# Hybrid decoder step on one Trainium2 core: dense projections as plain float32 matmuls instead of three split products

## The reference

```python
def layer(x, ...):
    h = rmsnorm(x, norm1_w)
    z = h @ w_in                     # 1024 -> 2 x 8 x 128 columns less 96: q, k, v, gates, latents, conv input
    y_ret = retention(...)           # 4 heads, chunks of 128, with a recurrent state
    y_mla = latent_attention(...)    # 8 heads; the 8 new tokens attend to 2048 cached positions in pages
    y_rg  = rg_lru(...)              # conv of width 4, gates, a scan
    x = x + concat([y_ret, y_mla, y_rg]) @ w_out          # 1024 -> 1024
    up = rmsnorm(x, norm2_w) @ w_up                       # 1024 -> 2 x 2816
    gate, val = split(up)
    x = x + (silu(causal_conv3(gate)) * val) @ w_down     # 2816 -> 1024
# after two layers: y = rmsnorm(x, final_w)
```

## Time and profile before

| | |
|---|---|
| median of 3 runs | 1723.7 us (1722.09 to 1728.46) |
| profiled execution, span | 1725.0 us |
| PE busy | 1541.2 us, 89% |
| weight loads busy | 1390.6 us, 81% |
| DVE busy | 882.3 us, 51% |
| ACT busy | 532.0 us, 31% |
| HBM read | 141.24 MB |
| mean granted TensorE clock | 0.895 |

### The profile page before, as it was taken

How to read it: one execution, slowest core, us unless ns; L and a number is a source line. 1 busy time by engine, 2 the same in 40 slices (tenths; PEclk the granted TensorE clock), 3 DMA queues, 4 the chain that set the end, 5 groups by cost and what they waited for, 6 DMA issues and landing times.

```text
span 1725.0 us, 31192 instructions
## 1 busy us (share of the span) xinstructions
PE 1541.2 (89%) x11052; PEld 1390.6 (81%) x11052; DVE 882.3 (51%) x1454; ACT 532.0 (31%) x778; POOL 24.7 (1%) x49
## 2 busy tenths in 40 slices
PE   4988797778999999999999888878899999999993
PEld 4988565446999999999998786544588999999993
DVE  4584142433476653666566812443336666356664
ACT  3340022322344422333423301222224443223341
POOL 1000000000000000000000000000000000000001
PEclk9996576889999999999999955778899999999997
DMA  7310212123222223222352012222232222232221
GB/s 274 117 56 26 82 49 79 45 68 98 89 71 86 89 85 107 85 97 71 106 185 89 21 55 65 69 59 70 72 105 73 89 87 82 95 99 87 79 92 50
DMA packets 119422, 146.72 MB, mean 85 GB/s; under 512 B 16609, under 2 KB 90626, under 8 KB 119202
## 3 DMA queue, kind: packets, MB, share of 16 engines
q1 hardware_dynamic: 116114, 133.54, 24.5%
q0 software_dynamic: 3216, 12.00, 2.0%
HBM read 141.24 MB, written 4.45 MB: 84 GB/s over the span
## 4 chain that ended last, share of the span: by engine, by line
PE 78%; DVE 8%; issue 7%; ACT 3%; SPq 2%; DMA 1%; DVEq 0%; ACTq 0%; POOL 0%; POOLq 0%
PE PS L1230 56%; PE PS L1508 4%; PE PS L1334 4%; PE PS L1459 2%; PE PS L1531 2%; PE PS L1332 1%; SPq L336 1%; SPq L341 1%; DVE STAT L1022 1%; PE PS L1245 1%; PE PS L1445 1%; PE PS L1383 1%; PE PS L1386 1%; ACT PR L643 1%; DVE R L840 1%
## 5 line engine op out<-in xcount | busy, mean ns | idle before, releaser
L1230 PE MATMUL PS<-XNH,WH 128*128 128x260 f32 x2176 | 445.7, 286 | 48.3 <-DVE WL L739 33.2
L1230 PE MATMUL PS<-XNH,WL 128*128 128x260 f32 x2176 | 442.6, 285 | 0.0
L1230 PE MATMUL PS<-XNL,WH 128*128 128x260 f32 x2176 | 442.1, 285 | 0.0
L1230 PEld LDWEIGHTS PS<-XNH,WH 128*128 128x128 f32 x2176 | 339.2, 190 | 52.4 <-issue 38.2
L452 ACT ACTIVATE WH<-RAW 128x1024 fp32r<-128x1024 f32 x200 | 211.5, 1058 | 435.7 <-PE PS L1230 360.2
L1230 PEld LDWEIGHTS PS<-XNH,WL 128*128 128x128 f32 x2176 | 338.4, 190 | 0.3
L1230 PEld LDWEIGHTS PS<-XNL,WH 128*128 128x128 f32 x2176 | 337.8, 190 | 0.4
L739 DVE TENSOR_TENSOR WL<-RAW,WH 128x1024 fp32r<-128x1024 f32 x200 | 244.5, 1222 | 168.7 <-ACT WH L452 162.3
L1230 PE MATMUL PS<-HL,WH 128*128 128x260 f32 x704 | 141.9, 283 | 0.0
L1230 PE MATMUL PS<-HH,WL 128*128 128x260 f32 x704 | 141.5, 282 | 0.0
L1230 PE MATMUL PS<-HH,WH 128*128 128x260 f32 x704 | 141.3, 282 | 0.0
(11 more groups left out here) (246 smaller groups left out, 1453.9 us busy)
## 6 DMA issues: line engine op xcount, KB each, us to landing
RAW<-in_units SPq DMA_DIRECT2D x134, 512.0 KB, 3.3
KT<-in_kat SPq DMA_DIRECT2D x256, 64.0 KB, 1.8
KT<-in_ka SPq DMA_DIRECT2D x256, 64.0 KB, 1.9
RAW<-in_units SPq DMA_DIRECT2D x32, 384.0 KB, 3.0
RAW<-in_units SPq DMA_DIRECT2D x32, 320.0 KB, 2.9
RT<-in_kar SPq DMA_DIRECT2D x256, 16.0 KB, 1.7
C<-in_const POOLq DMA_DIRECT2D x1, 2228.0 KB, 10.1
X<-in_x SPq DMA_DIRECT2D x8, 260.0 KB, 4.3
```

What stands on the lines that cost most here:

```text
L1230: last = mm(PS[i % 4][0:rows, hb, 0:HB], w, x(kk)[:, hb * HB:(hb + 1) * HB], start=(kk == 0 and s == 0), stop=(kk == total - 1 and s == 2))
```

## The change

The dense projections are done by plain float32 matmuls on the raw weights: two per weight tile and chunk instead of six. WH, WL, XNL and HL are gone, XNH becomes XN, HH becomes H, and RAW becomes W with seven slots. `hi` and `lo` and all the subtractions are removed. SP loads a unit when the product seven units back is done (UNIT_USE names the tile that uses a unit). The buffers that lay over the raw slots and the split buffers (PD, O8, SMALL, C8, QD, SS, KC) have places of their own. The first product and the first up product wait for XN chunk by chunk, the first down product of a half for each H tile. ACT alone empties the mixed outputs. The layer loops and inner loops are unrolled in Python, and CREDIT is gone.

```diff
-NRAW, NHL = 4, 2
+NW_SLOTS = 7
+UNIT_USE = [(f"in{z}", None) for z in ORDER] + [(f"wo{m}", None) for m in range(KD)]
+for _i, (_j0, _n) in enumerate(HALVES):
+    UNIT_USE += [(f"up{_i}_{j}", None) for j in range(2 * _n)]
+    for _m in range(KD):
+        UNIT_USE += [(f"dn{_i}_{_m}", KD * _i + _m + 1), (f"dn{_i}_{_m}", None)]
...
+        def wait_weights(e, l, u):
+            n = l * N_UNITS + u
+            e.wait_ge(w_full[n % NW_SLOTS], 16 * (n // NW_SLOTS + 1))
+
+        def wait_unit_used(e, l, u):
+            name, half = UNIT_USE[u]
+            if half is None:
+                wait_full(e, l, name)
+            else:
+                wait(e, "mid_used", l, half)
...
             def one(l, u, width=UW):
-                unit_wait(l, u)
-                src = units[bass.ds(l * N_UNITS + u, 1), :, 0:width].rearrange("a p n -> p (a n)")
-                sp.dma_start(RAW[:, u % NRAW, 0:width], src).then_inc(raw_full[u % NRAW], 16)
+                n = l * N_UNITS + u
+                if n >= NW_SLOTS:
+                    wait_unit_used(sp, *divmod(n - NW_SLOTS, N_UNITS))
+                sp.dma_start(W[:, n % NW_SLOTS, 0:width], units[n, :, 0:width]).then_inc(w_full[n % NW_SLOTS], 16)
...
-            with sp.Fori(0, DEPTH) as l:
-                for u in range(NRAW + 1):
+            for l in range(DEPTH):
+                for u in range(4):
                     one(l, u)
...
-                for u in range(NRAW + 1, N_IN_U + 2):
+                for u in range(4, N_IN_U):
                     one(l, u, 256 if u == U_KR else UW)
-                    g = u - (NRAW + 1)
+                    g = u - 4
                     if g < 2 * (N_PAGES // 4):
                         four_pages(l, 0, 0, g // 4, 4 * (g % 4))
-                with sp.Fori(0, NB // 2 - 1) as bp:
+                for u in range(N_IN_U, N_IN_U + NW_SLOTS):
+                    one(l, u)
+                for bp in range(NB // 2 - 1):
                     pages(l, 0, bp + 1)
-                with sp.Fori(0, NB // 2) as bp:
+                for bp in range(NB // 2):
                     pages(l, 1, bp)
-                wait_full(sp, l, "dy")
-                settle(sp)
-                for u in range(N_IN_U + 2, U_UP[0]):
+                for u in range(N_IN_U + NW_SLOTS, U_UP[0]):
                     one(l, u)
...
-            def hi(l, u, it=None, tile=None, mid=None):
...
-                act.activation(WH[:, u % NHL, :], RAW[:, u % NRAW, :], ACT.Copy).then_inc(hi_split[u % NHL], 1)
...
-            def lo(l, u, it=None, per=0):
...
-                V_.tensor_tensor(WL[:, u % NHL, :], RAW[:, u % NRAW, :], WH[:, u % NHL, :].bitcast(F32), ALU.subtract)\
-                    .then_inc(lo_split[u % NHL], 1)
...
-                remainder(l, c0, k, weight)
-
-            def remainder(l, c0, k, weight):
-                wait(dve, "xh_ready", l, c0 + k + 1)
-                V_.scalar_tensor_tensor(XNL[:, k, :], X[:, k, :], weight, XNH[:, k, :].bitcast(F32), ALU.mult, ALU.subtract)\
-                    .then_inc(S["xl_ready"][0], 1)
...
-                        act.activation(XNH[r, 2 + g // 2, 0:SEQ], ps(f"o{g}")[r, 0, :], ACT.Copy).then_inc(S["mix_hi"][0], 1)
+                        act.activation(XN[r, 2 + g // 2, 0:SEQ], ps(f"o{g}")[r, 0, :], ACT.Copy).then_inc(emptied(f"o{g}"), 1)
...
-                            V_.scalar_tensor_tensor(two(HF[:, jj, :]), two(TH[:, jj, :]), 0.5, PS[vi % 4][:, :, 0:HB],
+                            V_.scalar_tensor_tensor(two(H[:, it * 2 + jj, :]), two(TH[:, jj, :]), 0.5, PS[vi % 4][:, :, 0:HB],
                                                     ALU.mult, ALU.mult).then_inc(emptied_s[vi % 4], 1)
-                            lo(l, U_UP[hf] + 2 * jj + 3, it, 4)
-                            wait(dve, "hh_ready", l, c + 1)
-                            hsl = bass.ds(it * 2 + jj, 1)
-                            V_.tensor_tensor(HL[:, hsl, :], HF[:, jj:jj + 1, :], HH[:, hsl, :].bitcast(F32), ALU.subtract)\
-                                .then_inc(S["hl_ready"][0], 1)
...
+            def product(l, name, us, x, rows=P, ready=None):
+                wait_tile(pe, l, name)
+                total, kk = sum(n for _, n in us), 0
                 for u, n in us:
...
+                    wait_weights(pe, l, u)
+                    slot = (l * N_UNITS + u) % NW_SLOTS
                     for k in range(n):
...
-                        for s, (w, x) in enumerate(((wh, xh), (wh, xl), (wl, xh))):
-                            for hb in range(2):
-                                last = mm(PS[i % 4][0:rows, hb, 0:HB], w, x(kk)[:, hb * HB:(hb + 1) * HB],
-                                          start=(kk == 0 and s == 0), stop=(kk == total - 1 and s == 2))
+                        if ready is not None:
+                            ready(kk)
+                        for hb in range(2):
+                            last = mm(ps(name)[0:rows, hb, 0:HB], W[:, slot, k * rows:(k + 1) * rows],
+                                      x(kk)[:, hb * HB:(hb + 1) * HB], start=(kk == 0), stop=(kk == total - 1))
                         kk += 1
...
-            with pe.Fori(0, DEPTH) as l:
+            for l in range(DEPTH):
...
-                    product(l, f"in{ORDER[u]}", [(u, KD)], xh, xl, 32 if u == U_KR else P, norm=None if u else 0)
+                    product(l, f"in{ORDER[u]}", [(u, KD)], xn, 32 if u == U_KR else P,
+                            None if u else lambda k: wait(pe, "xn_ready", l, k + 1))
...
+                    for j in range(2 * n):
+                        product(l, f"up{hf}_{j}", [(U_UP[hf] + j, KD)], xn,
+                                ready=None if hf or j else lambda k: wait(pe, "xn_ready", l, KD + k + 1))
+                    for m in range(KD):
+                        u = U_DN[hf] + 2 * m
+                        product(l, f"dn{hf}_{m}", [(u, n // 2), (u + 1, n // 2)], lambda k: H[:, k, :],
+                                ready=None if m else lambda k: wait_emptied(pe, l, f"up{hf}_{2 * k + 1}"))
```

More of the change, by code:

```diff
@@ L21 @@
 F32 = mybir.dt.float32
-F32R = mybir.dt.float32r
 I32 = mybir.dt.int32
@@ L164, in build @@
         X = over("X", [P, KD, T])
[L165 to L172, removed]
+        xn0 = cursor[0]
+        XN = over("XN", [P, KD, T])
+        W = over("W", [P, NW_SLOTS, UW])
+        PD = over("PD", [P, NB * N_PAGES * MH])
+        O8 = over("O8", [MH, NB * P])
+        SMALL = over("SMALL", [P, 10, 64])
+        C8 = over("C8", [NB, P])
+        mix0 = cursor[0]
+        QD = over("QD", [P, 2, 512])
+        SS = over("SS", [P, 4, 2 * HD])
+        cursor[0] = mix0
+        KCs = [over(f"KC{i}", [96, 2, SEQ]) for i in range(2)]
+        VT = over("VT", [P, 4, 256], at=xn0)
+        KW = over("KW", [P, 4, 256], at=xn0 + 6 * T * 4)
+        QCs = [over(f"QC{i}", [96, 2, SEQ], at=xn0 + i * 6 * T * 4) for i in range(2)]
         C = over("C", [P, CONST_N])
@@ L209, in build @@
         K8V8 = over("K8V8", [NB, 512], at=gbase + 16384)
[L211 to L220, removed]
         cursor[0] = base
-        HH = over("HH", [P, 12, T], F32R)
-        HL = over("HL", [P, 12, T], F32R)
+        H = over("H", [P, 12, T])
         GB = over("GB", [P, 2, T + 8])
@@ L376, in _ @@
                                  (U_UP[1], 2 * HALVES[1][1], UW), (U_DN[1], 2 * KD, 5 * P)):
[L377 to L380, removed]
-                            row = l * N_UNITS + it * NRAW + (u0 + j)
-                            sp.dma_start(RAW[:, (u0 + j) % NRAW, 0:w],
-                                         units[bass.ds(row, 1), :, 0:w].rearrange("a p n -> p (a n)"))\
-                                .then_inc(raw_full[(u0 + j) % NRAW], 16)
+                    for u in range(u0, u0 + n):
+                        one(l, u, w)
         @block.gpsimd
@@ L684, in _ @@
                     t0 = TILE_AT[f"up{hf}_0"]
-                    with act.Fori(0, n // 2) as it:
+                    for it in range(n // 2):
                         for jj in range(2):
@@ L784, in _ @@
                 chunk(None, 0, k, NW[:, k:k + 1])
-            with dve.Fori(0, DEPTH) as l:
+            for l in range(DEPTH):
                 lay[0] = l
@@ L1101, in _ @@
                 V_.memset(ACC, 0.0).then_inc(S["acc_zero"][0], 1)
-                with dve.Fori(0, KD // 4) as it:
+                for it in range(KD // 4):
                     wait(dve, "acc_zero", l, 1)
@@ L1122, in _ @@
                     t0 = TILE_AT[f"up{hf}_0"]
-                    with dve.Fori(0, n // 2) as it:
+                    for it in range(n // 2):
                         for jj in range(2):
@@ L1204, in _ @@
             mm = nc.tensor.matmul
-            def product(l, name, us, xh, xl, rows=P, it=None, per=0, norm=None, chunks=None):
-                i = TILE_AT[name]
-                a = l * NT4 + i // 4 + CREDIT
-                pe.wait_ge(emptied_s[i % 4], a if it is None else a + it)
-                total = sum(n for _, n in us)
-                kk = 0
```

(8 more changed lines are left out.)

169 lines of the change are left out of this document (38 added, 131 removed).

## The result

| | before | after |
|---|---|---|
| median | 1726.1 us (1722.1 to 1729.5) | 1894.8 us (1894.2 to 1897.9) |
| span of the profiled execution | 1725.0 us | 1892.2 us |
| mean granted clock | 0.895 | 0.916 |

The ratio is 1.0975, with a 95% interval of 1.0951 to 1.0999: 9.75% slower. The forecast was 1904 us (1882 to 1935). The median of before is over four executions here, over the first three of them it was 1723.7.

A forecast was written before the change was run, and what follows sets the result against it. The prediction took PE's dense matmul stream plus a latency-bound middle stage as the bound. 1725.0 + 218.9 for dearer blocks - 39.0 for vanished waits and clock falls gave 1904.9, set to 1904 us by before's median; range 1882 to 1935.

The forecast's parts named there:

- the waits for WL: PE waiting for DVE's weight subtractions, 33.2 us in six waits; all to vanish, the four inside stages worth 5.1 us.
- 4/3: Block of float32 matmuls as four passes at the reduced pace: 0.964 us, +347 us, total 2032 us; chance 0.03.

The follow-up runs named there:

- the last kernel: Kernel before, loops unrolled, unit 0 split early, last input tiles emptied before two subtractions, unit 17's put behind the copies feeding page scores: 1696.7 us, ratio 0.981.

## What to carry over

A float32 matmul can be priced from eight records of it in the trace, by their spacing and not by their duration. An edit that seems to be mere form, as loops unrolled along the way, is to be priced by itself, first of all in a stage made of short waits; here it was worth 21 us by itself, beside gains of 54 in all, and hid in the same diff as a loss of 221. When a large edit brings side gains, ask which of them can be had without it: here 30 of the 54 us, by the last kernel's span. And when a wait vanishes from a list, look whether it stands at the same instruction under another name: four of the waits for WL did.

## What the runs showed of the hardware

Three records, one form each: reduced, 260 columns, 120.5 ns; float32, 260 columns, 219.2 ns; float32, 130 columns, 112.3 ns. In all of them a weight load of 190 ns goes with each record and stays hidden. A block of one float32 product thus costs 1.21 of one of three reduced products, not 4/3.

The granted clock after nearly the same wait isn't always the same. PE waits 2.4 us for DVE ahead of each n2 (2.6 in before, and with splits it waits once more behind n2, for XNL). In after all that follows is at full clock; with the split-like work put back, with nothing changed near n2, it is at the lower level. Sums by stage of after, then of the kernel with the work put back (columns as above):

```profile
476.00:478.50 2.50, 2.50 (x14) 2.15 (x13) 0.70 (x1) 2.50 (x5) 0.00 (x0) 1.00 0.00 0
```
```profile
482.80:485.00 2.20, 2.20 (x6) 1.69 (x6) 0.70 (x1) 2.20 (x4) 0.00 (x0) 0.51 0.00 0
```

14 records in 2.5 us against 6 in 2.2. It fell behind n2 in both layers of the kernel before and of the one with the work put back, in layer 1 alone with the loops alone unrolled, in layer 0 alone with four matmuls of 130 columns, and in neither layer of after and with four slots. What decides it wasn't tried and stays open; with the work put back it costs 1.7 us each time, from n2 to the next n1 or the end of the layer.
